# Scoring cached K pages in units of four pages instead of two, from one buffer of turned pages

## What is computed

```
def _fox_attend(q, fq, qpos, k, v, fk, kpos):
    s = jnp.einsum('nqhd,nkhd->nhqk', q, k).astype(jnp.float32) * (HEAD_DIM ** -0.5)
    s = s + (jnp.transpose(fq, (0, 2, 1))[:, :, :, None]
             - jnp.transpose(fk, (0, 2, 1))[:, :, None, :])
    mask = kpos[None, :] <= qpos[:, None]
    s = jnp.where(mask[None, None], s, -jnp.inf)
    p = jax.nn.softmax(s, axis=-1)
    return jnp.einsum('nhqk,nkhd->nqhd', p.astype(v.dtype), v)
...
            k_past = cache_k[page_table].reshape(nb, -1, N_HEADS, HEAD_DIM)
            v_past = cache_v[page_table].reshape(nb, -1, N_HEADS, HEAD_DIM)
```

## Time and profile before

| | |
|---|---|
| median of 3 runs | 963.65 us (963.64 to 964.45) |
| the profiled run | 964.55 us, of which the span in the profile is 962.7 us |
| PE matmuls | 928.9 us busy, 96% of the span |
| DVE, ACT, POOL | 500.0, 384.0 and 189.1 us busy |
| turns of K pages, L1211 | 1024 matmul records, 136.4 us |
| scores of K pages, L1414 | 1024 matmul records, 68.6 us in two groups |
| clock granted to PE | full in all 40 slices |

### The profile page before, as it was taken

The page is one execution under the profiler, slowest core; times in us unless marked ns, Lnnn a source line. Parts: engine busy times, 40 slices in busy tenths (PEclk is TensorE's granted clock), DMA queues, the critical chain, the costliest instruction groups (busy, mean ns, idle before and its releaser), DMA issues.

```text
span 962.7 us, 23462 instructions
## 1 busy us (share of the span) xinstructions
PE 928.9 (96%) x8356; PEld 789.5 (82%) x8356; DVE 500.0 (52%) x1133; ACT 384.0 (40%) x728; POOL 189.1 (20%) x143
## 2 busy tenths in 40 slices
PE   4999999999999999999999999999999999999998
PEld 4999999999998997758768678687687786775898
DVE  5774455556355434563654554645645546536632
ACT  5333333322135443543543544635444445346210
POOL 2234433342030221112102212111121022000000
PEclk9999999999999999999999999999999999999999
DMA  7233322224343526889799699798996997987412
GB/s 235 67 88 87 87 69 83 83 69 119 126 154 125 162 59 206 279 296 354 236 364 335 233 388 305 257 380 259 325 348 230 374 329 241 381 305 251 145 45 99
DMA packets 133333, 206.41 MB, mean 214 GB/s; under 512 B 8847, under 2 KB 91456, under 8 KB 133170
## 3 DMA queue, kind: packets, MB, share of 16 engines
q1 hardware_dynamic: 121602, 198.35, 61.0%
q10 hardware_dynamic: 11168, 5.51, 2.1%
q0 software_dynamic: 528, 2.10, 0.8%
HBM read 195.29 MB, written 10.63 MB: 214 GB/s over the span
## 4 chain that ended last, share of the span: by engine, by line
PE 80%; DMA 7%; ACT 4%; DVE 4%; SPq 3%; issue 3%; ACTq 0%; DVEq 0%
PE psum L1231 41%; PE psum L1211 16%; PE psum L1280 9%; PE psum L1414 7%; DMA page_ring<-in_cache_k 4%; ACT sample_scores L717 2%; PE psum L1524 2%; SPq L376 2%; SPq L378 1%; PE psum L1456 1%; DMA w_raw<-in_a_w_out 1%; DMA residual<-in_x_prompt 1%; PE psum L1329 1%; PE psum L1437 1%; DMA page_ring<-in_cache_v 1%
## 5 line engine op out<-in xcount | busy, mean ns | idle before, releaser
L1231 PE MATMUL psum<-xn_high,w_high 128*128 128x256 f32 (+1 forms) x992 | 237.0, 318 | 2.4 <-DVE w_low L842 2.4
L1231 PE MATMUL psum<-xn_low,w_high 128*128 128x256 f32 (+1 forms) x992 | 215.8, 297 | 0.0
L1231 PE MATMUL psum<-xn_high,w_low 128*128 128x256 f32 (+1 forms) x992 | 215.8, 297 | 0.0
L1231 PEld LDWEIGHTS psum<-xn_high,w_high 128*128 128x128 f32 x992 | 163.2, 191 | 29.7 <-issue 26.3
L1231 PEld LDWEIGHTS psum<-xn_high,w_low 128*128 128x128 f32 x992 | 168.4, 190 | 0.0
L1231 PEld LDWEIGHTS psum<-xn_low,w_high 128*128 128x128 f32 x992 | 168.3, 190 | 0.0
L1211 PE MATMUL psum<-constants,page_ring 128*128 128x128 f32 x1024 | 136.4, 276 | 3.7 <-DMA page_ring<-in_cache_k 2.5
L1211 PEld LDWEIGHTS psum<-constants,page_ring 128*128 128x128 f32 x1024 | 114.1, 141 | 29.2 <-issue 27.7
L502 POOL TENSOR_TENSOR w_raw<-w_raw,gains 128x1024 f32<-128x1024 f32 x32 | 60.7, 1897 | 343.2 <-DMA w_raw<-in_b_w_in 221.0
L1019 DVE COPY k_turned_odd<-psum 128x512 f32<-128x512 f32 x64 | 44.2, 690 | 93.1 <-PE psum L1211 93.1
L842 DVE TENSOR_TENSOR w_low<-w_raw,w_high 128x1024 fp32r<-128x1024 f32 x32 | 52.4, 1637 | 72.1 <-ACT w_high L575 72.1
(11 more groups left out here) (233 smaller groups left out, 1473.3 us busy)
## 6 DMA issues: line engine op xcount, KB each, us to landing
page_ring<-in_cache_k SPq DMA_DIRECT2D x128, 512.0 KB, 5.9
page_ring<-in_cache_v SPq DMA_DIRECT2D x128, 512.0 KB, 5.2
w_raw<-in_a_w_in SPq DMA_DIRECT2D x30, 512.0 KB, 4.0
suffix<-suffix_scratch SPq DMA_DIRECT2D x32, 256.0 KB, 4.6
w_raw<-in_b_w_in SPq DMA_DIRECT2D x16, 512.0 KB, 5.9
w_raw<-in_kv_w SPq DMA_DIRECT2D x16, 512.0 KB, 6.5
w_raw<-in_a_w_out SPq DMA_DIRECT2D x4, 1024.0 KB, 5.0
f_broad<-f_scratch SPq DMA_DIRECT2D x8, 512.0 KB, 6.5
```

Of the source, the lines that this page charges most:

```text
L1231: mm = pe.matmul(PS[:, bank + h, 0:c.stop - c.start], w[:, k, :], x[:, k, c], start=(k == 0 and n == 0), stop=(k == KT - 1 and n == 2))
```

## The change

A unit is four pages and 512 keys, one whole PSUM bank. There is one buffer of four turned pages in the place of the two of two pages; `PTS` now shares the second half of it. `unit_scores` runs behind the turns of pages 4, 8 and 12, ahead of the projection piece there, and the fourth unit stands where the eighth stood. ACT and DVE wait at pages 4, 8 and 12 for the score of the unit that lies in the buffer before they copy the new page, and DVE adds the suffix sums of 512 keys right after its copy. The suffix loads are issued ahead of steps 6, 10, 14 and 18 of SP's page stream instead of 4, 8, 12 and 16, each when the unit that read the slot has been added. The score banks count six a round instead of eight, and the waits on them are renumbered throughout.

```diff
-    KTS = [place("k_turned", [P, KT, 2 * PAGE])]
-    PTS = place("p_turned", [P, NPG, P])
-    KTS.append(place("k_turned_odd", [P, KT, 2 * PAGE], over=at["p_turned"]))
+    KTS = place("k_turned", [P, KT, 4 * PAGE])
+    PTS = place("p_turned", [P, NPG, P], over=at["k_turned"] + 4 * KT * 2 * PAGE)
...
@@ SP, heads
-                if n in (4, 8, 12, 16):
-                    c = n // 4 + 1
+                if n in (6, 10, 14, 18):
+                    c = (n - 6) // 4 + 2
                     if not (last and c >= 4):
-                        sp.wait_ge(b_c1f, 8 * i + n // 4)
+                        sp.wait_ge((b_c0f, b_c1f)[c % 2], 6 * i + c // 2)
                         load_suffix(i + c // 4, c % 4)
...
@@ POOL, heads
-                pool.wait_ge(b_c1, 8 * i + 4)
+                pool.wait_ge(b_c1, 6 * i + 2)
...
@@ ACT, heads
             for k in range(NPG):
-                c = (k % 2) * PAGE
-                if k % 2 == 0 and k >= 4:
-                    act.wait_ge((b_c0, b_c1)[k // 2 % 2], 8 * i + k // 4)
-                turned0(KTS[k // 2 % 2][:, 0:4, c:c + PAGE],
+                c = (k % 4) * PAGE
+                if k % 4 == 0 and k >= 4:
+                    act.wait_ge((b_c0, b_c1)[(k // 4 - 1) % 2], 6 * i + (k // 4 - 1) // 2 + 1)
+                turned0(KTS[:, 0:4, c:c + PAGE],
                         PS[:, T0, :].rearrange("p (k n) -> p k n", k=4)).then_inc(b_t0f, 1)
...
@@ DVE, heads
                 dve.tensor_tensor_reduce(
-                    SS[:, u * 256:(u + 1) * 256], PS[:, bank, 0:256],
-                    SFX[:, (u // 2) % 2, (u % 2) * 256:(u % 2) * 256 + 256],
+                    SS[:, u * 512:(u + 1) * 512], PS[:, bank, :], SFX[:, u % 2, :],
                     1.0, NEG, ALU.add, ALU.max, TINY[:, 4 + u:5 + u]).then_inc(free, 1)
 
             for k in range(NPG):
-                c = (k % 2) * PAGE
-                if k % 2 and k >= 3:
-                    u = k // 2 - 1
-                    if u % 2 == 0:
-                        dve.wait_ge(b_sfx[(u // 2) % 2], (2 * i + u // 4 + 1) * 16)
-                    dve.wait_ge((b_c0, b_c1)[u % 2], 8 * i + u // 2 + 1)
+                c = (k % 4) * PAGE
+                u = k // 4 - 1
+                if k % 4 == 0 and k >= 4:
+                    dve.wait_ge(b_sfx[u % 2], (2 * i + u // 2 + 1) * 16)
+                    dve.wait_ge((b_c0, b_c1)[u % 2], 6 * i + u // 2 + 1)
...
-                turned1(KTS[k // 2 % 2][:, 4:8, c:c + PAGE],
+                turned1(KTS[:, 4:8, c:c + PAGE],
                         PS[:, T1, :].rearrange("p (k n) -> p k n", k=4)).then_inc(b_t1f, 1)
-                if k % 2 and k >= 3:
-                    add_suffix(k // 2 - 1)
+                if k % 4 == 0 and k >= 4:
+                    add_suffix(u)
...
-            dve.wait_ge(b_c1, 8 * i + 4)
-            add_suffix(NPG // 2 - 1)
+            dve.wait_ge(b_c1, 6 * i + 2)
+            dve.wait_ge(b_sfx[1], (2 * i + 2) * 16)
+            add_suffix(3)
...
-            ch.link(dve.tensor_reduce(TINY[:, 12:13], TINY[:, 4:12], AX, ALU.max))
+            ch.link(dve.tensor_reduce(TINY[:, 12:13], TINY[:, 4:8], AX, ALU.max))
...
@@ PE, heads
-                pe.wait_ge(free, 8 * i + u // 2)
-                pe.wait_ge(b_t0f, 24 * i + 2 * u + 2)
-                pe.wait_ge(b_t1f, 24 * i + 2 * u + 2)
+                pe.wait_ge(free, 6 * i + u // 2)
+                pe.wait_ge(b_t0f, 24 * i + 4 * u + 4)
+                pe.wait_ge(b_t1f, 24 * i + 4 * u + 4)
                 for pp in range(2):
                     for j in range(4):
-                        mm = pe.matmul(PS[32 * j:32 * j + 32, bank, 0:256], QC[:, 2 * j + pp, :],
-                                       KTS[u % 2][:, 2 * j + pp, :],
+                        mm = pe.matmul(PS[32 * j:32 * j + 32, bank, :], QC[:, 2 * j + pp, :],
+                                       KTS[:, 2 * j + pp, :],
                                        start=(pp == 0), stop=(pp == 1), tile_position=(0, 32 * j))
...
+                if k % 4 == 0 and k >= 4:
+                    unit_scores(k // 4 - 1)
                 if k < 6:
                     project(0, ([0, 1], [2, 3], [4], [5], [6], [7])[k])
                 if 7 <= k < 15:
                     project(1, [k - 7])
-                if k % 2 == 0 and k >= 2:
-                    unit_scores(k // 2 - 1)
...
             project(2, [0])
-            unit_scores(NPG // 2 - 1)
+            unit_scores(NPG // 4 - 1)
             project(2, [1])
```

More of the change, by code:

```diff
@@ L404, in heads @@
                 if n == 0:
-                    sp.wait_ge(b_c0f, 8 * i)
-                    sp.wait_ge(b_c1f, 8 * i)
+                    sp.wait_ge(b_c0f, 6 * i)
+                    sp.wait_ge(b_c1f, 6 * i)
                     src = f_dram[bass.ds(2 * i, 2), 0:SEQ].unsqueeze(0).to_broadcast([P, 2, SEQ])
@@ L521, in heads @@
                 if r:
-                    pool.wait_ge(b_c0f, 8 * i + 4 + r)
-                    pool.wait_ge(b_c1f, 8 * i + 4 + r)
+                    pool.wait_ge(b_c0f, 6 * i + 2 + r)
+                    pool.wait_ge(b_c1f, 6 * i + 2 + r)
                 pool.tensor_tensor(own, own, CT[:, C_CM:C_CM + P].unsqueeze(1).to_broadcast([P, 2, P]),
@@ L526, in heads @@
             if not last:
-                pool.wait_ge(b_c1, 8 * i + 4)
+                pool.wait_ge(b_c1, 6 * i + 2)
                 pool.tensor_copy(QC[:, :, :].rearrange("p k n -> p (k n)"),
                                  QZ[:, bass.ds(i + 1, 1), :, :].rearrange("p a k n -> p (a k n)")).then_inc(b_qc, 1)
-                pool.wait_ge(b_c0, 8 * i + 8)
-                pool.wait_ge(b_c1, 8 * i + 8)
+                pool.wait_ge(b_c0, 6 * i + 6)
+                pool.wait_ge(b_c1, 6 * i + 6)
                 pool.tensor_copy(QT[:, :], QF[:, bass.ds(i + 1, 1), 0:SEQ].rearrange("p a n -> p (a n)")).then_inc(b_qt, 1)
@@ L1053, in heads @@
             dve.wait_ge(s_fnr, 1)
-            dve.wait_ge(b_c1, 8 * i + 4)
-            add_suffix(NPG // 2 - 1)
-            dve.wait_ge(b_c0f, 8 * i + 4)
-            dve.wait_ge(b_c1f, 8 * i + 4)
+            dve.wait_ge(b_c1, 6 * i + 2)
+            dve.wait_ge(b_sfx[1], (2 * i + 2) * 16)
+            add_suffix(3)
+            dve.wait_ge(b_c0f, 6 * i + 2)
+            dve.wait_ge(b_c1f, 6 * i + 2)
             cq = CQ[:, bass.ds(i, 1)]
             ms = MS[:, bass.ds(i, 1)]
-            ch.link(dve.tensor_reduce(TINY[:, 12:13], TINY[:, 4:12], AX, ALU.max))
+            ch.link(dve.tensor_reduce(TINY[:, 12:13], TINY[:, 4:8], AX, ALU.max))
             ch.link(dve.tensor_tensor(ms, TINY[:, 12:13], cq, ALU.add))
@@ L1074, in block_max @@
                 c = 20 + 20 * (r % 2)
-                dve.wait_ge(b_c0, 8 * i + 4 + r + 1)
-                dve.wait_ge(b_c1, 8 * i + 4 + r + 1)
+                dve.wait_ge(b_c0, 6 * i + 2 + r + 1)
+                dve.wait_ge(b_c1, 6 * i + 2 + r + 1)
                 if r >= 2:
@@ L1086, in block_max @@
                 dve.wait_ge(b_fq, 4 * i + r + 1)
-                dve.wait_ge(b_c0f, 8 * i + 4 + r + 1)
-                dve.wait_ge(b_c1f, 8 * i + 4 + r + 1)
+                dve.wait_ge(b_c0f, 6 * i + 2 + r + 1)
+                dve.wait_ge(b_c1f, 6 * i + 2 + r + 1)
                 ch.link(dve.tensor_tensor(TINY[:, c + 2:c + 4], TINY[:, c:c + 2], fq, ALU.add))
@@ L1450, in block_scores @@
                 w = (s + 1) * P
-                pe.wait_ge(b_c0f, 8 * i + 4 + r)
-                pe.wait_ge(b_c1f, 8 * i + 4 + r)
+                pe.wait_ge(b_c0f, 6 * i + 2 + r)
+                pe.wait_ge(b_c1f, 6 * i + 2 + r)
                 heads2 = ((slice(0, 64), C0, b_c0), (slice(64, 128), C1, b_c1))
@@ L1535, in _ @@
         pe.wait_ge(b_kst, NB)
-        pe.wait_ge(b_c0f, 8 * NB)
-        pe.wait_ge(b_c1f, 8 * NB)
+        pe.wait_ge(b_c0f, 6 * NB)
+        pe.wait_ge(b_c1f, 6 * NB)
         pe.wait_ge(b_gf, NB)
```

## The result

The changed kernel takes 967.97 us (median of 15 runs), the kernel before 964.14 in as many: a ratio of 1.0034, 95% interval 1.0022 to 1.0045. It is slower by 0.34%, where 0.4% faster was forecast; the range ended at 965.0.

A forecast was written before the change was run, and what follows sets the result against it. TensorE's step list in the K stage was taken as the bound. Per round 1.09 - 0.64 - 0.02 = 0.43 us, 3.4 in eight, gave 960.2 us against 963.65 (chance 0.54); range 956.2 to 965.0.

The forecast's parts named there:

- SP and DMA: Suffix loads issued later in SP's page stream: the fourth's issue fits, its transfer is 0.63 us at most, taken as 0.
- Rival C: Moved suffix load delays the next round's first K page, 0.63 us at seven joints, 4.4 in all: 964.6; chance 0.12.
- Scoring: PE's score units in the K stage: three of 2.06 us replace seven of 1.16, the last grows 0.85; saves 1.09 a round.
- D: Score units on PE: 512 columns take twice 256, 2.21 us a unit; within 0.2%, 965.0; chance 0.10.
- E: Score units on PE: weight loads (16, 1.76 us), not columns, set the 1.00; net 0.99 us a round, 955.7; chance 0.12.
- Pages 6 and 7: PE's turn 7 directly follows turn 6 in the same two banks and stalls 0.64 us a round, 5.1 in all.
- One buffer: Pages 4, 8, 12: copies wait for the score; T0 free 0.89 after the piece begins, next turn after 0.90; taken as 0.
- B: Turns 5, 9 and 13 wait behind ACT's copy, 24 times 0.28 us, 6.7 in all: slower, 966.9; chance 0.12.
- The rule of the Trainium skill: Emptying pages 4, 8 and 12 cannot overlap scoring: by it alone 0.89 us is exposed 24 times, 981.6.
- Page 15: Projection after turn 15 waits for ACT's copy, 0.18 us late; the old order lost 0.16 a step later: +0.02 a round.

## Why the prediction was wrong, and where it was right

**The step that failed** is the one on SP and DMA: "Its 256 KB go out about 679 to 680, when 225 GB/s move, while 690 to 691 moves 414: 0.63 us of transfer at most, and I take 0." That SP has the time for the issue was right, since its next K page goes out as early as before. The transfer was wrong twice. I read 225 GB/s against 414 as a hole of 46%. The same row gives the DMA engines' share as 0.78: nearly four fifths of their time was taken, at a lower rate. The hole was in bytes, not in time; over the stretch the engines had 0.80 us idle, and 0.65 stayed idle with the load there. And 0.63 prices the load at the rate of pages; it cost 0.7 (moved alone, 4.95/7) to 0.9 us a joint. Rival C named the load and that it delays the pages, with too small a price, a chance of 0.12 and a sign that does not show it: the wait for the first K page is still 0.35, and the delay stands in the waits for the V pages ahead of it. With 0.83 a joint, and the 0.33 measured in the K stage, C gives 963.65 - 8 x 0.33 + 7 x 0.83 = 966.8, outside the range and near the measured time.

**Scoring, right.** A unit was forecast at 0.18 + 1.85 + 0.03 over a plain page; the rows show 0.96 going in (0.97), 1.86 (1.85), 0.89 going out (0.90). The slope from the block scores carried over, and D and E fall. One small term was missed: turn 5 takes 0.82 to its piece, not 0.79, three times a round. E's 1.76 us of weight loads counts sixteen loads one behind the other. Windows of the score line, a unit of 256 keys before and one of 512 after (span, PE, weight loads, clock, DMA share, GB/s):

```profile
652.47:653.48 1.01, 1.01 (x16) 0.42 (x16) 1.00 0.92 233
```

```profile
640.49:642.35 1.86, 1.86 (x16) 0.42 (x16) 1.00 1.15 333
```

Loads are under way for 0.42 us of either, so halving their number could save 4 x 0.42 = 1.7 us a round at most, not 7.0. That 1.76 does not fit into 1.00 therefore says nothing; but 256 more columns in both rounds cost 0.86, so by that slope only 0.14 of the old 1.00 lies outside the columns, and most of the 0.42 overlaps matmuls.

**Pages 6 and 7, right.** 2.24 us against the 2.22 worked out, released by ACT as said; of the 0.3 and 0.6 us that were expected in the K stage, the two kernels that turn page 7 elsewhere gain 0.29 and 0.48 (47.20 and 47.01 against 47.49).

**One buffer, right.** ACT's copies after, timeline: page 4 (after its score) and page 6.

```profile
642.56 0.60 ACT L675 ACTIVATE k_turned<-psum 128x512 f32<-128x512 f32 x1 [3.48 <-PE psum L1412]
...
645.58 0.60 ACT L675 ACTIVATE k_turned<-psum 128x512 f32<-128x512 f32 x1 [1.07 <-PE psum L1209]
```

The copy of page 4 starts 0.21 after the piece (0.23 forecast) and ends at 643.16; turn 5 starts at 643.24 without a wait. ACT sees the end of the longer score no later than DVE saw that of the shorter one; B, the rival that said slower, falls, and the kernel is slower for another reason. The rule of the Trainium skill (Perfetto Trace Analysis, Optimizing Tensor Performance, Matmuls) that groups should rotate through banks was weighed there. The trace shows nothing of its price at pages 4, 8 and 12, where a piece covers the copy; at pages 6 and 7, where none does, it shows 0.66 us a round.

**Page 15, right.** PE timeline after: piece 14, turn 15, the next projection's piece, the last unit.

```profile
664.10 0.51 PE L1229 MATMUL psum<-xn_high,w_high 128*128 128x256 f32 x2
...
664.98 1.03 PE L1209 MATMUL psum<-constants,page_ring 128*128 128x128 f32 x8
665.95 0.53 PE L1229 MATMUL psum<-xn_high,w_high 128*128 128x256 f32 x2
...
666.93 1.92 PE L1412 MATMUL psum<-k_turned,q_current 128*32 128x512 f32 x16
```

The piece comes 1.85 after piece 14 (1.66 + 0.18 = 1.84), the score 0.98 later.

In all a round's K stage gained 0.33 us where 0.43 was forecast; with the moved load undone, the kernel is 0.32% faster (0.9968), where 960.2 against 963.65 was 0.36%. The interval, 0.14% to 0.51%, cannot tell these from the 0.27% that 8 x 0.33 us are, so the agreement is in part luck.

## What to carry to other kernels

When a change moves a transfer, price it in the time of the DMA engines in the stretch where it lands, by their busy share and by what loads of that form cost, not by its bytes at the best rate; a stretch with few GB/s can be full. Where the order of issues is free, put small loads ahead of the wait that opens a dense stretch, not behind it: here that choice of two steps decided the sign of the whole change. And where single buffers are to be hidden, look for the one place in the cycle that has no filler work, and give that place its own bank: here that took 0.29 us off each K stage, though the whole time fell clear of the noise only when the pieces were moved as well.

## What the runs showed of the hardware

I had not expected that its bytes say so little of what a load costs: in the V stretch one suffix load of 256 KB (128 rows of 2 KB, from 16 rows read eight times) cost 0.88 us a joint and one page of 512 KB 0.85, with SP on time in both. Nor does a full busy share mean one rate. Beside the suffix load the DMA engines moved 248 to 250 GB/s at a share of 1.0, and pages alone 393 at 0.98; but pages alone also moved only 229 at 0.99, at the place of the window from 682.40 above, in the run with the fourth load back:

```profile
675.00:676.00 1.00, 1.00 (x9) 0.51 (x7) 0.59 (x1) 0.57 (x1) 0.00 (x0) 1.00 0.99 229
```

So the suffix load is not all that lowers the rate there; what else does, no run here shows.
